# Row statistics taken on three columns per partition in three handovers, with the first modulation in halves and another order of the weight ring

## What is computed

```
h = _rmsnorm(x, pre_g) * (1 + sc) + sh          # sc, sh, gt: six slices of silu(c) @ ada_w + ada_b
y = sub_layer(h)
x = x + gt * _rmsnorm(y, post_g)
_rmsnorm(x, g) = x * rsqrt(mean(x * x) + 1e-6) * g
```

## Time and profile before

| | us |
|---|---|
| median of 3 runs | 1657.11 (1651.82 to 1658.64) |
| the profiled execution, its time | 1656.61 |
| the profiled execution, its span | 1654.5 |
| TensorE busy in the span | 1578.5 (95%) |
| VectorE busy | 1145.8 (69%) |
| ScalarE busy | 959.6 (58%) |
| mean granted TensorE clock | 0.983 |

### The profile page before, as it was taken

The page is one execution under the profiler, slowest core; times in us unless marked ns, Lnnn a source line. Parts: engine busy times, 40 slices in busy tenths (PEclk is TensorE's granted clock), DMA queues, the critical chain, the costliest instruction groups (busy, mean ns, idle before and its releaser), DMA issues.

```text
span 1654.5 us, 25672 instructions
## 1 busy us (share of the span) xinstructions
PE 1578.5 (95%) x10491; PEld 1330.6 (80%) x10491; DVE 1145.8 (69%) x1259; ACT 959.6 (58%) x1174; POOL 107.4 (6%) x193
## 2 busy tenths in 40 slices
PE   6999889989999998999889999999999999999997
PEld 3999467768999997996867888888888888888885
DVE  3865641586444456346668888888888888888887
ACT  2553423555333445326757777777777777777775
POOL 2211000000000000000011010100101010000021
PEclk9999999999999999999989999999999999999999
DMA  9820986479552559369329999999999999999995
GB/s 323 251 78 2 329 295 206 149 235 254 153 153 90 171 181 299 103 199 363 115 82 353 366 366 382 357 386 363 377 369 371 381 358 386 363 373 363 369 380 188
DMA packets 268790, 450.05 MB, mean 272 GB/s; under 512 B 12773, under 2 KB 125630, under 8 KB 268658
## 3 DMA queue, kind: packets, MB, share of 16 engines
q1 hardware_dynamic: 264312, 433.72, 75.7%
q0 software_dynamic: 3632, 13.11, 2.0%
q10 hardware_dynamic: 720, 1.50, 0.3%
HBM read 423.78 MB, written 24.51 MB: 271 GB/s over the span
## 4 chain that ended last, share of the span: by engine, by line
PE 46%; DVE 2%; DMA 1%; ACT 1%; issue 0%; SPq 0%; DVEq 0%; ACTq 0%
PE bank L428 14%; PE bank L430 14%; PE bank L429 14%; PE bank L2810 1%; DMA slot_rows<-gate_rows_far 1%; DVE w_lo_late L3050 1%; PE bank L2784 1%; PE bank L2732 0%; PE bank L2794 0%; ACT w_hi_late L2898 0%; DVE raw L3189 0%; PE bank L2725 0%; DVE raw L3183 0%; DVE xT L3178 0%; PE bank L2869 0%
## 5 line engine op out<-in xcount | busy, mean ns | idle before, releaser
L3050 DVE TENSOR_TENSOR w_lo_late<-raw,w_hi_late 128x2048 fp32r<-128x2048 f32 x262 | 598.5, 2291 | 102.0 <-ACT w_hi_late L2898 100.4
L2898 ACT ACTIVATE w_hi_late<-raw 128x2048 fp32r<-128x2048 f32 x262 | 502.5, 1918 | 156.7 <-PE bank L430 156.7
L428 PE MATMUL bank<-w_hi_late,hg_hi 128*128 128x512 f32 (+1 forms) x768 | 292.4, 381 | 1.7 <-ACT hg_hi L2915 0.9
L430 PE MATMUL bank<-w_hi_late,hg_lo 128*128 128x512 f32 (+1 forms) x768 | 289.4, 377 | 0.0
L429 PE MATMUL bank<-w_lo_late,hg_hi 128*128 128x512 f32 (+1 forms) x768 | 289.4, 377 | 0.0
L332 DVE TENSOR_TENSOR w_lo_main<-raw,w_hi_main 128x2048 fp32r<-128x2048 f32 (+1 forms) x50 | 112.4, 2249 | 89.8 <-ACT w_hi_main L324 89.8
L428 PEld LDWEIGHTS bank<-w_hi_late,hg_hi 128*128 128x128 f32 x768 | 144.6, 188 | 30.8 <-DVE w_lo_late L3050 1.2
L430 PEld LDWEIGHTS bank<-w_hi_late,hg_lo 128*128 128x128 f32 x768 | 144.6, 188 | 29.3
L429 PEld LDWEIGHTS bank<-w_lo_late,hg_hi 128*128 128x128 f32 x768 | 144.8, 188 | 28.0
L428 PE MATMUL bank<-w_hi_late,act_hi 128*128 128x512 f32 x352 | 142.1, 404 | 0.5 <-DVE w_lo_late L3050 0.4
L430 PE MATMUL bank<-w_hi_late,act_lo 128*128 128x512 f32 x352 | 139.6, 397 | 0.0
(11 more groups left out here) (553 smaller groups left out, 2801.7 us busy)
## 6 DMA issues: line engine op xcount, KB each, us to landing
raw<-in_moe_w_gate SPq DMA_DIRECT2D x88, 1024.0 KB, 7.2
raw<-in_moe_w_up SPq DMA_DIRECT2D x88, 1024.0 KB, 7.2
raw<-in_moe_w_down SPq DMA_DIRECT2D x88, 1024.0 KB, 6.6
ada_delta<-in_ada_w SPq DMA_DIRECT2D x32, 1024.0 KB, 7.3
raw<-in_gdn_w_in SPq DMA_DIRECT2D x16, 1024.0 KB, 10.2
slot_rows_far<-zero_row SPq DMA_DIRECT2D x1, 12288.0 KB, 39.1
raw<-in_ffn_w_gate SPq DMA_DIRECT2D x22, 512.0 KB, 4.4
raw<-in_ffn_w_up SPq DMA_DIRECT2D x22, 512.0 KB, 5.6
```

The source lines that it names most:

```text
L428: pe.matmul(out, w_hi, x_hi, start=start, stop=False)
L430: return pe.matmul(out, w_lo, x_hi, start=False, stop=stop)
L2898: act.activation(k.w_hi[:, m % SPL, :], k.raw[:, k.slot(m), :], ACT.Copy).then_inc(k.hi_ready, 1)
L3050: dve.tensor_tensor(k.w_lo[:, m % SPL, :], k.raw[:, k.slot(m), :], k.w_hi[:, m % SPL, :], ALU.subtract).then_inc(k.raw_split, 1)
```

## The change

In each handover the sums are made with the data as the stationary operand and one column of ones as the moving one, so that a sum is one number per token, on three columns of [128, 1] (tokens 0 to 127, 128 to 255, 192 to 319). VectorE combines on [128, 3]. ScalarE's logarithm is written out 128 times beside each other, a product with the identity spreads it to all rows of a bank, and the exponential is taken from there. The old sums move out of the last slab. VectorE works on the first tiles of x after the combination, not before. The units of the modulation groups move forward: one right after the last slab, one after the sums of y, one after the other sums, one after the last spread, and two ahead of the next stage's products in place of three within its first slab. The router's 16 shift products move into the third handover. The ring takes two ada slabs after slab 0 of the next stage and six after its slab 1. Group 0 is worked in halves: 4 slabs (shift and scale of tiles 0 to 3) in setup, the other 4 through `k.raw` in the next block, the last of them and their turn within the first slab. The convolution's 24 transposes become 2.

```diff
-    before = {first["ffn_up"] + AHEAD: ADA_EARLY, first["kv_w"] + AHEAD: ADA_EARLY + 1}
+    before = {first["ffn_up"]: ADA_EARLY, first["kv_w"]: ADA_EARLY + 1}
...
+        if n == first["w_in"] + 1:
+            order += [("ada", j) for j in range(ADA_GROUP // 2, ADA_GROUP)]
+        if n - 1 in before:
+            order += [("ada", ADA_GROUP * before[n - 1] + j) for j in range(2)]
+        if n - 2 in before:
+            order += [("ada", ADA_GROUP * before[n - 2] + j) for j in range(2, ADA_GROUP)]
...
+    def first_turn(self, pe, part):
+        pe.wait_ge((self.half_copied, self.ada_copied)[part], 1)
+        bank = (self.ps[0], self.ps[6])[part]
+        for q in range(4):
+            last = pe.matmul(bank[:, 8 * q:8 * q + 8], self.ada_rows[:, q * P:(q + 1) * P], self.ada_sum[:], start=True, stop=True)
+        last.then_inc((self.half_turned, self.ada_turned)[part], 1)
...
-        turns.append(([conv_rows[:, q * P:(q + 1) * P] for q in range(QKV_T)], 7, k.conv_cols[:]))
+        turns.append(([conv_rows[:, 0, :]], 4 * QKV_T, k.conv_cols[:, :, 0:4].rearrange("p q t -> p t q"), QKV_T))
+        turns.append(([conv_rows[0:3 * QKV_T, 1, :]], 3 * QKV_T, k.conv_cols[:, :, 4:7].rearrange("p q t -> p t q"), QKV_T))
...
 # setup_phase, sync
-            for n in range(ADA_GROUP - 1):
+            for n in range(ADA_GROUP // 2):
                 k.ada_load(sp, n)
-            k.load_through(sp, 0)
-            k.ada_load(sp, ADA_GROUP - 1)
-            k.load_through(sp, 2)
+            k.load_through(sp, ADA_GROUP // 2)
 # setup_phase, tensor: the order behind the transposes of x
-            k.ada_pe(pe, 2)
+            for n in range(2, 4):
+                k.first_pe(pe, n)
+            pe.wait_ge(small_in, 16 * len(loads))
+            for n in range(n_first, len(turns)):
+                turn(n)
             pe.wait_ge(diag_ready, 1)
+            k.first_turn(pe, 0)
...
-            k.ada_pe(pe, 4)
-            k.ada_pe(pe, 1)
 # Renewal.dve
         self.times(dve, 0)
-        run(grown_by(k, dve, slice(2, 4)))
         low(0)
 # mixed_phase, tensor
+            def column_sums(col, parts):
+                for t, t0 in enumerate(COLUMN_AT):
+                    for n, part in enumerate(parts):
+                        last = pe.matmul(col[:, t:t + 1], part[:, t0:t0 + P], k.ones[:, 0:1], start=(n == 0), stop=(n == len(parts) - 1))
+                return last
+            def spread_rows(n):
+                for t, t0 in enumerate(COLUMN_AT):
+                    last = pe.matmul(row_banks[n][:, t0:t0 + P], spread[:, t, :], k.ident[:], start=True, stop=True)
+                last.then_inc(sig["part"].sem, 1)
...
+            modulate(1)
             pe.wait_ge(sig["summed"].sem, summed0 + KT - 2)
-            pe.matmul(sum_bank, k.ones[:], y_sum, start=True, stop=False)
             pe.wait_ge(sig["squared"].sem, squared0 + KT)
-            pe.matmul(sum_bank, k.ones[:], k.squares[:, (KT - 1) % 2, :], start=False, stop=True).then_inc(sig["part"].sem, 1)
+            column_sums(sum_col, (y_sum, k.squares[:, (KT - 1) % 2, :])).then_inc(sig["part"].sem, 1)
             modulate(1)
+            pe.wait_ge(sig["root"].sem, root0 + 1)
+            spread_rows(0)
+            pe.wait_ge(sig["old"].sem, old0 + 2 * KT - 1)
+            column_sums(old_col, (old_sum,))
             pe.wait_ge(sig["crossed"].sem, crossed0 + KT)
-            pe.matmul(cross_bank, k.ones[:], cross_sum, start=True, stop=True)
+            column_sums(cross_col, (cross_sum,))
             pe.wait_ge(sig["grown"].sem, grown0 + KT - 1)
-            pe.matmul(grown_bank, k.ones[:], grown_sum, start=True, stop=True).then_inc(sig["part"].sem, 1)
-            modulate(2)
+            column_sums(grown_col, (grown_sum,)).then_inc(sig["part"].sem, 1)
+            if renewal.router:
+                renewal.sum_shift(pe)
+            modulate(1)
+            pe.wait_ge(sig["root"].sem, root0 + 4)
+            spread_rows(1)
+            modulate(1)
 # mixed_phase, scalar
+            def spread_log(col):
+                act.activation(spread, col.unsqueeze(2).to_broadcast([P, 3, P]), ACT.Ln, scale=1.0 / D,
+                               bias=k.eps[:]).then_inc(sig["root"].sem, 1)
             act.wait_ge(sig["part"].sem, part0 + 2)
-            run(act.activation(r_y, sum_bank, ACT.Ln, scale=1.0 / D, bias=k.eps[:]))
-            act.activation(r_y, r_y, ACT.Exp, scale=-0.5).then_inc(sig["root"].sem, 1)
+            spread_log(sum_col)
+            act.wait_ge(sig["root"].sem, root0 + 1)
+            act.activation(r_col, spread[:, :, 0], ACT.Exp, scale=-0.5).then_inc(sig["root"].sem, 1)
+            act.wait_ge(sig["part"].sem, part0 + 3)
+            act.activation(r_y, row_banks[0], ACT.Exp, scale=-0.5).then_inc(sig["root"].sem, 1)
             act.wait_ge(sig["crossed"].sem, crossed0 + KT + 1)
-            run(act.activation(k.rstd, cross, ACT.Ln, scale=1.0 / D, bias=k.eps[:]))
-            act.activation(k.rstd, k.rstd, ACT.Exp, scale=-0.5).then_inc(sig["root"].sem, 1)
+            spread_log(mean_col)
+            act.wait_ge(sig["part"].sem, part0 + 5)
+            act.activation(k.rstd, row_banks[1], ACT.Exp, scale=-0.5).then_inc(sig["root"].sem, 1)
 # mixed_phase, vector: the five operations stand on [128, 3]; grown_by(0:2), which was ahead of them, and add_grown(0:2) follow
+            dve.tensor_scalar(mean_col, mean_col, 0.0, None, ALU.max).then_inc(sig["crossed"].sem, 1)
+            dve.wait_ge(sig["root"].sem, root0 + 3)
+            run(grown_by(k, dve, slice(0, 2)))
+            add_grown(k, dve, slice(0, 2))
+            run(grown_by(k, dve, slice(2, 4)))
 # modulated
-        if s == 0 and KT <= step < KT + 3:
-            k.ada_pe(pe, 1)
 # conv_phase, tensor
+            def beside(s, step):
+                if s == 0 and step == KT:
+                    k.first_pe(pe, ADA_GROUP - 1)
+                if s == 0 and step == KT + 2:
+                    k.first_turn(pe, 1)
+                gate_products(s, step)
+            for n in range(ADA_GROUP // 2, ADA_GROUP - 1):
+                k.first_pe(pe, n)
 # conv_phase, scalar, in the loop over tiles
+                if kt == KT // 2 - 1:
+                    k.first_act(act, 1)
 # conv_phase, vector
+                if kt == KT // 2:
+                    low(kt - 1)
+                    k.first_dve(dve, 1).then_inc(k.ada_kept, 1)
+                    dve.wait_ge(k.ada_kept, 1)
+                    coefs(1)
 # copy_phase and ffn_up_phase, tensor, ahead of dense_tiles
+            k.ada_pe(pe, 2)
 # moe_phase, tensor: the 16 products are gone from its start
-            for s in range(2):
-                for kt in range(KT):
-                    last = pe.matmul(shift_sums[:, s, :], renewal.shift[:, kt, s:s + 1], k.w_router[:, kt, :], start=(kt == 0), stop=(kt == KT - 1))
-            last.then_inc(logits_done, 1)
```

More of the change, by code:

```diff
@@ L58 @@
 ADA_EARLY = 5
+FIRST_BLOCKS = (0, 2, 1, 3)
 class Signal:
@@ L364, in ada_arrived @@
         else:
-            pe.wait_ge(self.ada_full[n % (2 * SPL)], 16 * (n // (2 * SPL) + 1))
+            pe.wait_ge(self.ada_full[n % (2 * SPL)], 16 * sum(("ada", m) not in self.place for m in range(n % (2 * SPL), n + 1, 2 * SPL)))
     def ada_banks(self, g):
@@ L424, in ada_dve, with first_pe, first_act, first_dve @@
                 dve.tensor_tensor(mod, got, bias, ALU.add).then_inc(self.ada_kept, 1)
+    def first_pe(self, pe, n):
+        part, j = divmod(n, ADA_GROUP // 2)
+        block, half = FIRST_BLOCKS[n // 2], n % 2
+        bank = (self.ps[0], self.ps[7])[part]
+        self.ada_arrived(pe, n)
+        for q in range(KT // 2):
+            last = pe.matmul(bank[32 * q:32 * q + 32, :], self.c_pad[:, half * (KT // 2) + q, C_AT - 2 * block:C_AT - 2 * block + 32],
+                             self.ada_tile(n)[:, q, :], start=(j == 0), stop=(j == ADA_GROUP // 2 - 1))
+        last.then_inc(self.ada_read, 1)
+    def first_turn(self, pe, part):
[4 more added lines that the diff above has]
+        last.then_inc((self.half_turned, self.ada_turned)[part], 1)
+    def first_act(self, act, part):
+        act.wait_ge(self.ada_read, (part + 1) * ADA_GROUP // 2)
+        act.activation(self.ada_rows[:], (self.ps[0], self.ps[7])[part][:], ACT.Copy).then_inc((self.half_copied, self.ada_copied)[part], 1)
+    def first_dve(self, dve, part):
+        dve.wait_ge((self.half_turned, self.ada_turned)[part], 1)
+        bank, blocks = (self.ps[0], self.ps[6])[part], slice(part, 4, 2)
+        mod = self.mod[:, 0:16, :].rearrange("p (j q) s -> p q j s", q=4)[:, :, blocks, :]
+        bias = self.vec_a[:, 0:16].rearrange("p (j q) -> p q j", q=4)[:, :, blocks].unsqueeze(3).to_broadcast([P, 4, 2, 2])
+        got = bank[:, 0:32].rearrange("p (q j s) -> p q j s", q=4, j=4)[:, :, blocks, :]
+        return dve.tensor_tensor(mod, got, bias, ALU.add)
     def three(self, pe, out, w_hi, w_lo, x_hi, x_lo, start, stop):
@@ L565, in _ @@
             pe.wait_ge(cond_ready, 1)
```

(21 more changed lines are left out.)

96 lines of the change are left out of this document (46 added, 50 removed).

## The result

| | before | after |
|---|---|---|
| median of 14 runs | 1653.62 us (1649.08 to 1658.64) | 1657.39 us (1653.59 to 1663.68) |
| ratio to before, 95% interval | | 1.0026 [1.0015, 1.0036] |
| the profiled execution: time, span | 1656.61, 1654.5 | 1656.94, 1655.0 |
| mean granted TensorE clock | 0.983 | 0.984 |

The predicted time was 1657.3 and no change within 0.5%: that came true, and so did nearly the figure. But the shift was +3.8 us where +0.2 was forecast; that the figure fits is luck, because before's median fell from 1657.1 over 3 runs to 1653.6 over 14.

The account below looks back on a forecast made before the run. TensorE's chain, mostly expert products, was taken as the bound. Setup -2.3 and handovers +0.5, +1.4, +0.6 sum to +0.2, so 1656.8 against the profiled 1656.6; the median stands 0.5 higher, 1657.3 us, range 1649 to 1665.

Parts of the forecast that it names:

- The forecast case: Whole kernel: a gain in setup is spent again in the handovers, 1657.3 us, own range 1653 to 1661, chance 0.62.
- Setup, forecast -2.3: Setup up to slab 1 of the first projection: gain of 2.3 us, bounds 0 and -3.1, slab 1 at 48 to 50.
- If the clock falls in the diagonal products: Setup: on a clock fall these products cost up to twice 5.76 us and the gain of 3.1 is gone.
- so I keep its landing: Setup: the last ada slab still lands at 35.1 us, since the transfers ahead of it are the same in number.
- The price of a pass, 0.13: Handovers' column sums: 0.13 us a pass, because the moving side hardly matters; the 30 passes take 3.9.
- rival of cheap columns: Handovers: passes cost 0.03 us in place of 0.13, in all -11 with setup, 1646 us, chance 0.08.
- Second handover, forecast +1.4: Handover at 618 to 641 us: +1.0 at full clock, +1.4 with the clock allowance.
- bound by VectorE's three: Second handover: three VectorE operations of 0.82 us set the 2.8 from combination to the next block's first operation.
- First and third, forecast +0.5 and +0.6: Handovers at 360 to 386 and 831 to 849 us: -0.4 to 0 and +0.35 at full clock, before the clock allowance.
- I take a bit over a third of it: Handovers: part of the half-clock losses (up to 1.9, 1.2, 0.6 us) is counted, giving +0.5, +1.4, +0.6.
- rival of slow columns: Handovers: the clock stays at half through a whole handover, +17 with setup, 1674 us, chance 0.09.
- Full speed throughout: Setup and handovers at full clock: -3.1, -0.4, +1.0, +0.35 = -2.2, 1655 us, chance 0.21.

Follow-up runs that it names:

- experiment 8: The kernel before with only the convolution's 24 transposes made 2, and the load that goes with them; 1654.35 us, ratio to before 0.9996.
- experiment 9: The changed kernel with each column sum taken against 128 moving columns of ones in place of one, over four banks; 1653.05 us, ratio to before 0.9999.
- experiment 3: The changed kernel with only VectorE's order of before, first two tiles multiplied ahead of the combination; 1655.59 us, ratio to before 1.0010.
- experiments 5: The changed kernel with the three column products of the old sums moved ahead of the wait for y's sums; 1656.71 us, ratio to before 1.0011.
- experiment 6: The changed kernel with VectorE's order of before, old sums ahead of y's sums and four filler products in the third handover; 1657.96 us, ratio to before 1.0016.
- experiment 4: The changed kernel with five unused products of 512 columns in TensorE's waits of the third handover; 1655.11 us, ratio to before 1.0011.
- experiment 2: The changed kernel with row sums, VectorE's old order and the router's shift products back at its start; 1646.95 us, ratio to before 0.9958.
- 10: The changed kernel with 128 moving columns of ones in the column sums and VectorE's order of before; 1652.61 us, ratio to before 1.0005.
- experiment 7: The changed kernel with row sums and VectorE's order of before, the router's 16 shift products kept in the third handover; 1645.84 us, ratio to before 0.9947.
- experiment 1: The kernel before with the setup part alone (halves, 2 transposes, setup's ring order), handovers unchanged; 1646.1 us, ratio to before 0.9956.
- experiment 11: The experiment 7 kernel with three unused products of 512 columns behind the shift products in the third handover; 1647.02 us, ratio to before 0.9960.

## Why the prediction was right, and where it was not

The forecast case, a gain in setup spent again in the handovers, is what happened: alone the setup gains 0.44%, the columns cost 0.68%, and a loss of 0.26% is left. That is about -7 and +11 us; forecast were -2.3 and +2.5. The total held because both sides were too small, which is luck: the mechanism was right, the sizes were not.

**Setup, forecast -2.3, measured -4.8 at slab 1.** Slab 1's start at 46.5 lies outside the 48 to 50 that were named as the sign. The 2.5 that are missing are three pieces. 0.8 is the allowance under "If the clock falls in the diagonal products": they took 5.74, and no fall came. The reason given for it, the 24 small transposes, is in doubt too: without them the clock fell at the same place in experiment 8. 1.3 lies up to the fifth tile, whose high half ended at 39.8 and not 41.1: the step "so I keep its landing" carried the slab's 35.1 over, and it was there 1.1 sooner. 0.4 more came from there to slab 1. Another 1.2 came between slab 1 and the first handover and was not traced.

**The price of a pass, 0.13: right.** Twelve passes took 1.50, eighteen 2.07 to 2.11, 0.115 to 0.125 each. That ends the rival of cheap columns at its root. The Trainium skill, "TensorE: Matmul & The Clock Gate", section "LDWEIGHTS (loading the stationary operand)", would have 0.107; from start to start the passes of the trace stand 0.112 apart, nearer to it than the 0.13 taken. That a single moving column saves nothing on the load is what the trace and experiment 9 show.

**Second handover, forecast +1.4, measured +1.4.** The chain came out nearly as laid down: sums to combination 5.4 (forecast 5.7), five operations at 0.196 (0.21), 2.98 to the next block (2.8). That block opens 0.8 earlier than before with a lead of 3.0 spent down by 2.2 (forecast 2.4). But its last step had the wrong owner: "bound by VectorE's three" is refuted by experiment 3. The tails of ScalarE and TensorE, which the prediction let end "about there too", set it: spread, and the unit behind it. And the match to 0.1 is partly luck: the sum took +0.4 for a lower clock, while the stretch had 3.2 us at half clock against before's 6.4.

**First and third, forecast +0.5 and +0.6, measured +3.0 and +2.8: the step that failed.** It is "I take a bit over a third of it" for the clock. In the first handover half clock covers the unit behind the first sums with the first spread, and later the second spread with the last unit (unit 1.93 for 1.07, two spreads 1.65 for 0.94, unit 1.77): 3.0 us over full speed ahead of the next block, partly met by slack. In the third the 18 passes cost 3.85 for 2.07. The rival of slow columns had this mechanism, at 3.9 more for 30 passes; the second handover, at full clock, and the setup kept the total from it. "The clock stays at half through the sums" was named as a sign that the prediction is wrong, and the nine sums of the third handover showed it. Against that rival stood that the clock falls only after a wait; experiments 5 and 6 refute this, with falls behind 18 thin passes and no wait. Experiment 9's runs tie the lower clock to the single moving column, experiment 4 and the third handover of 9 tie it to the waits: either can do it. In the first stretch the table prices it at 0.4 us for each us at half clock.

**What the columns cost without the clock.** At 3 us low the first stretch takes 38.1 with columns and, in experiment 2 at 3.7 low, 36.9 with rows; the second takes 80.8 and 79.6 at the same 3.2. In the third it is 59.3 at 10.7 (experiment 6) against 57.2 at 10.3 (2), and 58.8 at 3.5 (10) against 56.1 at 3.4 (7). So 1.2, 1.2 and 2.1 to 2.7 are plain series work, about 5 us in all by single traces; against experiment 1, whose handovers are those of before, it is some 6. From the other side, widening the columns gave back 0.27%, 4.5 us, and experiment 9, with a clock as high as that of the row sums, still stands 0.41%, 6.8 us, above experiment 2. Of the 11 us, then, 4 to 7 are the longer series and 4 to 7 the clock; the runs don't divide them closer.

**Ring order and queues, forecast nothing:** nothing shows (experiments 1 and 2). **Full speed throughout,** the rival at 0.21, fell with the clock. **The bound of 0.5%** hid a loss that 14 runs tell apart: the change is 0.26% slower. Its setup is worth having: with row sums it is 0.4% faster than before in experiment 2, and 0.5% with the router's early shift products in experiment 7, whose own share doesn't show.

## What to carry to other kernels

Fewer elements for VectorE are no gain when TensorE must then load each data tile as the stationary side: here 1.47 us of combination were saved, and 3.3 of passes, spreads and a longer logarithm put into the same series, 0.7 of it moved there from the last slab. Split a change that touches several stretches and run its parts alone before judging it; a total near zero here was -7 and +11. And where a handover's clock varies from run to run, compare medians and intervals, and read the granted clock of each stretch beside its duration before explaining a difference of two traces.

## What the runs showed of the hardware that was not expected

- At full clock a product with a [128, 128] f32 stationary side and one moving column costs 0.115 to 0.125 us a pass, and one with 128 moving columns 0.12 to 0.13 (18 passes: 2.07 to 2.11 against 2.17; 12 passes: 1.50 against 1.60); from start to start it is 0.112 in both.
- Thin products don't hold TensorE's speed as wide ones do, at equal spacing of the passes: granted clock 0.984 over after's runs, 0.990 over experiment 9's. They can let it fall with no wait of TensorE: behind 18 in one run it fell in all four handovers that have such a run and no wait (experiments 5 and 6: 360.4, 619.8, 358.5 and 621.3), while in the first two handovers of experiments 9 and 10, also without a wait ahead of the sums, the wide passes kept it.
- A wait can do it without thin passes: in experiment 9's third handover it fell during the wide passes behind a wait of 2.2 us, and with five products of 512 columns in the waits (experiment 4) 18 thin passes ran at full clock, 2.07. In the changed kernel both stand together: it fell at 357.5, behind a wait of 1.30 and 12 thin passes, and at 832.0, as the run of 18 began, behind waits of 2.2 and 0.7; in its second handover, with 12 thin passes and no wait ahead of them, it held to 630.
- Filling the handover with products of 512 columns brought the time at half clock in the third stretch from 3.4 to 0 in experiment 11 and gained nothing that shows: there VectorE worked without a gap from 831.4 to 837.1 on renewing the tiles, and TensorE waited for ScalarE's output of them (0.66), so a faster TensorE has nothing to gain in it.
- A logarithm written out to 384 elements per partition from three took 0.58 to 0.61, one of 320 took 0.53 to 0.56: spreading by ScalarE is nearly free here. What costs is the product behind it, 0.94 at full clock, and the small exponential of three columns, 0.21, ahead of the wide one.
